# Four first products taken from the input without its norm's factor, with the input read first, in four blocks

## What is computed

```python
h = rms_norm(x, norm1_g[l])
z = h @ w_in[l].astype(h.dtype)
glu_in, q, k, v, gate_logits = jnp.split(z, SPLITS, axis=-1)
a_val, a_gate = jnp.split(glu_in, 2, axis=-1)
a = a_val * jax.nn.sigmoid(a_gate)
a = causal_depthwise_conv(a, conv_w[l], conv_b[l])
```

## Time and profile before

| | us |
|---|---|
| median of 3 runs | 908.16 |
| lowest, highest | 907.64, 909.5 |
| the profiled execution | 906.52 |
| its span in the trace | 904.7 |
| first product with a weight starts | 14.38 |
| first job of q reaches the sum of squares on PE | 97.23 |

### The profile page before, as it was taken

The page is one execution under the profiler, slowest core; times in us unless marked ns, Lnnn a source line. Parts: engine busy times, 40 slices in busy tenths (PEclk is TensorE's granted clock), DMA queues, the critical chain, the costliest instruction groups (busy, mean ns, idle before and its releaser), DMA issues.

```text
span 904.7 us, 18066 instructions
## 1 busy us (share of the span) xinstructions
PE 859.0 (95%) x6762; PEld 837.4 (93%) x6762; DVE 649.4 (72%) x1059; ACT 555.5 (61%) x999; POOL 350.5 (39%) x324
## 2 busy tenths in 40 slices
PE   4999889999999999999999989899999999999996
PEld 3998889999899899999999878799999999999996
DVE  5987999896777798777665659957577854444542
ACT  5677778887646576665555675456645655555441
POOL 3799995435432253333110215701032243333111
PEclk9999999999999999999999999999999999999999
DMA  5655444444565366665656443245345466654741
GB/s 201 209 187 186 162 144 151 137 132 140 151 184 186 111 189 205 186 180 175 214 163 194 160 142 110 82 136 166 115 143 172 150 211 188 182 180 152 217 133 47
DMA packets 42310, 146.41 MB, mean 162 GB/s; under 512 B 4704, under 2 KB 7024, under 8 KB 42224
## 3 DMA queue, kind: packets, MB, share of 16 engines
q1 hardware_dynamic: 41472, 143.67, 50.9%
q10 hardware_dynamic: 752, 1.59, 0.5%
...
## 4 chain that ended last, share of the span: by engine, by line
PE 72%; DVE 11%; issue 8%; POOL 6%; ACT 3%; DMA 1%; DVEq 0%; POOLq 0%; ACTq 0%
PE px L507 22%; PE px L508 22%; PE px L509 22%; DVE wlo L1316 3%; POOL CA L1876 2%; DVE px L1375 2%; POOL att L1996 1%; PE px L549 1%; PE px L571 1%; ACT whi L843 1%; DVE sq L1331 1%; POOL wlo L1827 1%; DVE Q L1406 1%; DMA X<-xs 1%; ACT hx L870 1%
## 5 line engine op out<-in xcount | busy, mean ns | idle before, releaser
L507 PE MATMUL px<-hx,whi 128*128 128x256 f32 x1392 | 404.4, 291 | 9.2 <-DVE hx L1337 6.1
L509 PE MATMUL px<-hx,wlo 128*128 128x256 f32 x1392 | 396.6, 285 | 0.0
L508 PE MATMUL px<-hx,whi 128*128 128x256 f32 x1392 | 396.6, 285 | 0.0
L1316 DVE TENSOR_TENSOR wlo<-raw,whi 128x1024 fp32r<-128x1024 f32 x251 | 330.8, 1325 | 65.0 <-ACT whi L843 64.6
L843 ACT ACTIVATE whi<-raw 128x1024 fp32r<-128x1024 f32 x267 | 279.9, 1051 | 65.0 <-PE px L509 49.8
L507 PEld LDWEIGHTS px<-hx,whi 128*128 128x128 f32 x1392 | 269.7, 194 | 14.2 <-DVE hx L1337 7.4
L508 PEld LDWEIGHTS px<-hx,whi 128*128 128x128 f32 x1392 | 270.0, 194 | 0.4
L509 PEld LDWEIGHTS px<-hx,wlo 128*128 128x128 f32 x1392 | 269.7, 194 | 0.0
L1950 POOL TENSOR_TENSOR fx<-tt,fx 128x256 fp32r<-128x256 f32 x40 | 54.3, 1359 | 130.1 <-ACT fx L1104 130.1
L1876 POOL TENSOR_TENSOR CA<-CA,ct 128x256 f32<-128x256 f32 x90 | 85.7, 953 | 45.5 <-ACT ct L910 37.9
L508 PE MATMUL px<-fx,whi 128*128 128x256 f32 x352 | 99.6, 283 | 0.0
...
## 6 DMA issues: line engine op xcount, KB each, us to landing
raw<-ws SPq DMA_DIRECT2D x267, 512.0 KB, 3.7
...
```

The source lines that it names most:

```text
L507: e.matmul(b[:, 0:S], H, xh, start=first, stop=False)
L508: e.matmul(b[:, 0:S], H, xl, start=False, stop=False)
L509: m = e.matmul(b[:, 0:S], L, xh, start=False, stop=end)
L1316: e.tensor_tensor(wlo[:, n % NSL, :], raw[:, n % NRAW, :], whi[:, n % NSL, :], ALU.subtract).then_inc(s_lov, 1)
```

## The change

The factor 1 / rms is taken out of the first four jobs. ACT makes `ax` high = round(X * gain), DVE the low half, and ag0, av0, ag1, av1 use `ax` in place of `hx`. When rst is there, DVE multiplies their results by it (`early`), and forms the gated tiles in a second step (`early_gated`). `hx` is made as before, for the jobs from ag2 on.

The input is stored as four blocks of two tiles, which SP loads ahead of all else. Chunks 0 and 1 are loaded and split in halves of 512 columns. Of the vector of small constants the first 9 columns come by themselves (through ACT's queue), the rest after chunk 2. Chunk 3's low half moves from POOL to DVE. PE runs 20 products of ones by ones (128 columns, type f32) before its first job; nobody reads the result. The norm's sum on PE stands after av0.

```diff
-s_x = [sem("s_x0"), sem("s_x1")]
+s_x = [sem(f"s_x{i}") for i in range(4)]
 def on_gpsimd(c):
-    return c < 64 and c % 4 == 3
+    return 4 <= c < 64 and c % 4 == 3
...
# PE
+e.wait_ge(s_con, 1)
+for _ in range(WARM):
+    e.matmul(px[VALUES[0]][:, 0:P], ones[:, :], ones[:, :], start=True, stop=True, skip_group_check=True)
+job(("ag", 0), AX, first_gained, rings=(FEW,))
+job(("av", 0), AX, rings=(FEW,))
 sums("n1")
-for i in range(KD):
-    job(("ag", i), HX, normed("n1") if i == 0 else None, rings=(FEW,))
+job(("ag", 1), AX, rings=(FEW,))
+job(("av", 1), AX, rings=(FEW,))
+for i in range(2, KD):
+    job(("ag", i), HX, normed("n1") if i == 2 else None, rings=(FEW,))
     job(("av", i), HX, rings=(FEW,))
...
# ACT
+e.dma_start(vc[:, 0:FIRST_VECS], vecs[:, 0:FIRST_VECS]).then_inc(s_vg, 16)
 e.preload_act_table_set(LOG)
...
 for i in range(KD):
+    if i % 2 == 0:
+        e.wait_ge(s_x[i // 2], 16)
+    e.activation(ax[:, i, 0, :], X[:, i, :], ACT.Copy, scale=vec("norm1_g", i)).then_inc(s_xgh, 1)
+    if i == 5:
+        half_high(0, 0)
+half_high(0, 1)
...
 rms("n1", D)
+def early_gate(i):
+    e.wait_ge(*BANK[("ag", i), 0])
+    e.activation(sg[:, i, :], sg[:, i, :], ACT.Tanh, scale=0.5).then_inc(s_eg, 1)
+early_gate(0)
+highs(4)
+early_gate(1)
+e.wait_ge(s_vc, 16)
+for i in range(KD):
+    e.wait_ge(s_nt, i + 1)
+    e.activation(hx[:, i, 0, :], sq[:, nt_slot("n1", i), :], ACT.Copy).then_inc(s_nhi, 1)
     if i == 4:
+        highs(5)
...
# DVE
+e.wait_ge(s_vg, 16)
+for i in range(KD):
+    e.wait_ge(s_xgh, i + 1)
+    e.scalar_tensor_tensor(out=ax[:, i, 1, :], in0=X[:, i, :], scalar=vec("norm1_g", i), in1=ax[:, i, 0, :],
+                           op0=ALU.mult, op1=ALU.subtract).then_inc(s_xgl, 1)
+    if i == 5:
+        half_low(0, 0)
+half_low(0, 1)
+half_low(1, 0)
+half_low(1, 1)
+lows(2)
...
+def early(key, to):
+    e.wait_ge(s_mm, ENDS[key])
+    e.tensor_tensor(to, px_of[key, 0][:, 0:S], rst[:, 0, 0:S], ALU.mult).then_inc(BANK[key, 0][0], 1)
...
# SP
-e.dma_start(X[:, 4:8, :], xv[:, 4:8, :]).then_inc(s_x[1], 16)
+for i in range(4):
+    tiles(i)
+half_load(0, 0)
+half_load(0, 1)
+half_load(1, 0)
+half_load(1, 1)
+loads(2)
+e.dma_start(vc[:, FIRST_VECS:], vecs[:, FIRST_VECS:]).then_inc(s_vc, 16)
```

More of the change, by code:

```diff
@@ L374, in two_blocks @@
         MX = CX + pairs(mh3, 3)
-        s_x = [sem("s_x0"), sem("s_x1")]
+        s_x = [sem(f"s_x{i}") for i in range(4)]
+        s_vg, s_half = sem("s_vg"), [sem(f"s_half{i}") for i in range(HALVED)]
         s_vc, s_wg2, s_caus, s_msk, s_pos, s_out = (sem(n) for n in (
@@ L423, in on_gpsimd, with steps, half, gated_half @@
         def on_gpsimd(c):
-            return c < 64 and c % 4 == 3
+            return 4 <= c < 64 and c % 4 == 3
+        def steps(c):
+            return 2 if c < HALVED else 1
         LOW = {}
         for c in range(n_chunks):
-            n = c // 4 if c < 64 else 16
-            LOW[c] = (s_log, c // 4 + 1) if on_gpsimd(c) else (s_lov, c + 1 - n)
+            mine = [d for d in range(c + 1) if on_gpsimd(d) == on_gpsimd(c)]
+            LOW[c] = (s_log if on_gpsimd(c) else s_lov, sum(steps(d) for d in mine))
+        HI = [sum(steps(d) for d in range(c + 1)) for c in range(n_chunks)]
+        def half(h):
+            return slice(h * CW // 2, (h + 1) * CW // 2)
+        def gated_half(i):
+            return (s_ci, i + 1) if i < 2 else BANK[("av", i), 0]
         ACC = {i: px[3][:, S * (n % 2):S * (n % 2) + S] for n, i in enumerate(CONV_V)}
@@ L456, in two_blocks @@
         QR = [qraw[:, 12 + n, :] for n in range(4)]
-        xv = x.rearrange("p (k s) -> p k s", k=KD)
+        xv = [x[i * P:(i + 1) * P, :].rearrange("p (k s) -> p k s", k=2) for i in range(KD // 2)]
         outv = out.rearrange("p (k s) -> p k s", k=KD)
@@ L498, in job @@
                     c, o = (at_ + k * w) // CB, (at_ + k * w) % CB * P
-                    if c != seen[0]:
+                    if c < HALVED and o in (0, CW // 2):
+                        e.wait_ge(s_lov, 2 * c + 1 + (o > 0))
+                    elif c >= HALVED and c != seen[0]:
                         seen[0] = c
@@ L832, in _, with half_high @@
         def _(e):
-            made = [0]
+            made = [HALVED]
+            def half_high(n, h):
+                e.wait_ge(s_raw[n] if h else s_half[n], 16)
+                e.activation(whi[:, n, half(h)], raw[:, n, half(h)], ACT.Copy).then_inc(s_hi, 1)
             def highs(c):
@@ L1303, in _, with half_low @@
         def _(e):
-            made = [0]
+            made = [HALVED]
+            def half_low(n, h):
+                e.wait_ge(s_hi, 2 * n + h + 1)
+                e.tensor_tensor(wlo[:, n, half(h)], raw[:, n, half(h)], whi[:, n, half(h)], ALU.subtract).then_inc(s_lov, 1)
             def lows(c):
@@ L1312, in lows @@
                         continue
-                    e.wait_ge(s_hi, n + 1)
+                    e.wait_ge(s_hi, HI[n])
                     if n >= NSL:
@@ L1359, in _, with early_gated @@
             e.tensor_scalar(qg8[:, :], vec("qg"), 0.125, None, ALU.mult).then_inc(s_cst, 1)
-            norm("n1", X, "norm1_g", hx)
+            lows(3)
+            def early(key, to):
+                e.wait_ge(s_mm, ENDS[key])
+                e.tensor_tensor(to, px_of[key, 0][:, 0:S], rst[:, 0, 0:S], ALU.mult).then_inc(BANK[key, 0][0], 1)
+            def early_gated(i):
+                e.wait_ge(s_eg, i + 1)
+                e.wait_ge(*BANK[("av", i), 0])
+                e.scalar_tensor_tensor(out=CI[:, i, 30:], in0=sg[:, i, :], scalar=1.0, in1=CI[:, i, 30:], op0=ALU.add,
+                                       op1=ALU.mult).then_inc(s_ci, 1)
+            e.wait_ge(s_rms, 1)
+            early(("ag", 0), sg[:, 0, :])
+            early(("av", 0), CI[:, 0, 30:])
+            scaled("n1", 0, X[:, 0, :], "norm1_g")
+            early(("ag", 1), sg[:, 1, :])
+            for i in range(1, KD):
+                scaled("n1", i, X[:, i, :], "norm1_g")
+                low_tile("n1", i - 1, hx)
+                if i == 3:
+                    lows(4)
+                elif i == 5:
+                    early_gated(0)
+            low_tile("n1", KD - 1, hx)
+            early(("av", 1), CI[:, 1, 30:])
+            lows(5)
+            early_gated(1)
             def taps(c):
@@ L1382, in _ @@
                 taps(2 * i + 1)
[L1383 to L1386 removed]
+                if i >= 2:
+                    e.wait_ge(*BANK[("ag", i), 0])
+                    e.wait_ge(s_mm, ENDS["av", i])
+                    e.scalar_tensor_tensor(out=CI[:, i, 30:], in0=sg[:, i % 3, :], scalar=1.0,
+                                           in1=px_of[("av", i), 0][:, 0:S], op0=ALU.add, op1=ALU.mult).then_inc(
+                                               BANK[("av", i), 0][0], 1)
             for n in range(2):
@@ L2039, in table, with tiles, half_load @@
                 e.dma_start(tb[:, h % 3, :], tabs[h]).then_inc(s_tb[h % 3], 16)
-            e.dma_start(X[:, 4:8, :], xv[:, 4:8, :]).then_inc(s_x[1], 16)
+            def tiles(i):
+                e.dma_start(X[:, 2 * i:2 * i + 2, :], xv[i]).then_inc(s_x[i], 16)
+            def half_load(n, h):
+                e.dma_start(raw[:, n, half(h)], ws[n][:, half(h)]).then_inc(s_raw[n] if h else s_half[n], 16)
+            for i in range(4):
[6 more added lines that the diff above has]
+            e.dma_start(vc[:, FIRST_VECS:], vecs[:, FIRST_VECS:]).then_inc(s_vc, 16)
             loads(ahead(last_chunk(QKG[9])) + NRAW)
```

63 lines of the change are left out of this document (34 added, 29 removed).

## The result

| | before | after |
|---|---|---|
| median | 907.78 us | 913.01 us |
| lowest, highest | 906.73, 909.5 | 912.25, 915.43 |
| the profiled execution's span | 904.7 | 911.2 |
| first product with a weight | 14.38 | 8.82 |
| first tap on POOL | 34.70 | 37.97 |

The changed kernel is slower: ratio 1.0061, 95% interval 1.0046 to 1.0077, or 5.2 us. PE starts 5.6 us earlier, and the kernel ends later. Only 9 of the 124 are as short as before's profiled execution (906.52); their common median is 909.03. So a shift against that one trace looks up to 2.5 us worse than one against a usual execution of before.

A forecast was written before the change was run, and what follows sets the result against it. POOL, then DVE, bound the kernel up to 131.5 us, not PE, so POOL's first tap sets the end. Variants +1.6 and +2.8 gave a middle of 2.2: 908.16 + 2.2 = 910.4 us, range 905.5 to 913.0.

The forecast's parts named there:

- 1.6 for the taps: POOL's first tap at 36.5 instead of 34.7, 1.8 later, 1.6 with 0.2 taken off, passed on to the end.
- 0.6 for half of a low clock at the start: Clock falling in PE's wait behind av0 puts the end at +2.8 instead of +1.6; the middle, 2.2, was taken.
- Input and ACT: Span's start: first `ax` at 3.9, chunk 2's high half at 11.9, its low half at 13.1, additions ending at 16.1.
- the idle time behind av0: PE, from 13.4 to 16.1: it waits 2.7 us for the norm's additions.
- From rst to POOL's last low tile: Norm tiles on ACT, DVE and POOL: from rst at 18.2 to the last low tile at 29.2, instead of 20.07.
- the row by which the forecast went: ACT's profile row: table load 1.28 us, tanh 0.01 after it; the skill's further 1.38 drain would give 911.8.
- The 0.2 us taken off for POOL's one wait: POOL's single 0.4 us wait for ACT: about 0.2 isn't its ordinary tap step, so the end moves that much less.
- The clock at the start: PE's 2.7 us wait behind av0: if the clock falls, sum and ag1 lose some 1.5 us, ACT hides 0.3.
- PE at 97 us: PE's wait ahead of `hsq`: longer than before, first `hsq` product at 98.8 or later instead of 97.23.
- PE's gain getting through: Faster rival, chance 0.15: POOL has unseen slack, PE's 2.6 us gain at av3 remains, 905.6, down to 904.2.
- Warm products that don't warm: Slower rival, chance 0.07: low clock for ag0 and av0, 10.2 us not 5.8; end 2.7 later than forecast, 913.1.
- Nothing is left either way: Rival, chance 0.18: POOL and DVE hold each other up; another phase can give back one or two us, 908.2.

The follow-up runs named there:

- the 124: Executions of the unchanged kernel before, timed 124 times on four chips beside the follow-up experiments; medians 908.53 to 909.23 us, common median 909.03.
- the one with 14 products filled in: Changed kernel with 14 unread products of ones on PE ahead of its first `hsq` product: 910.31 us against 909.23 for before, ratio 1.0015.
- three kernels: 14 products filled in: changed kernel 1.0015 (unfilled 1.0061), with norm's chain first 0.9975 (0.9991), with chain and POOL's memsets first 0.9968 (0.9994).

## Why the prediction was too low

The direction and the core hold: PE's start gives nothing, POOL's first tap is late, and its delay reaches the end whole. The time is 913.01 where 910.4 was forecast, with 913.0 as the upper end. The forecast's 2.2 us were 1.6 for the taps and 0.6 for half of a low clock at the start. Measured are 3.3 for the taps, none for the second term in the profiled execution, and a rest that the forecast has no term for. Step by step:

- *Input and ACT.* First `ax` at 3.70 (forecast 3.9). But a rounding with the gain costs 0.40 us in a row, not 0.31, the third block came at 5.83 instead of 5.1 and the first half piece at 7.32 instead of 6.3. So chunk 2's high half ends at 13.1 instead of 11.9, its low half at 14.36 instead of 13.1, the additions end at 17.34 instead of 16.1, `rst` at 19.55 instead of 18.2. **This term was mis-sized by 1.35 us.** On 0.40: the Trainium skill, "ScalarE: Activation LUTs", What ACT_TABLE_LOAD costs, gives 93 ns for each per-partition operand; 0.31 and 0.09 make the 0.40 of the trace.
- *PE.* ag0 starts at 8.82 (7.6 to 8.7), and the idle time behind av0 is 2.83 us (2.7).
- *From rst to POOL's last low tile.* 11.1 us (11.0). The table load takes 1.28 us and tanh starts 0.01 us behind it, as in the row by which the forecast went.
- *POOL.* The memsets 4.9 and the low half 2.4 as counted. 37.97 instead of 36.5, which is `rst`'s delay. The 0.2 us taken off for POOL's one wait wasn't there: 3.3 at the first tap, 3.4 at 126 us.
- *The clock at the start.* In this execution it stayed up at the sum and fell at 26.3. In others it fell at the sum (at 17.0 in the one with 14 products filled in), and the first tap came at 39.15, 1.2 later: the step that the forecast priced at 1.2 and took half of.
- *PE at 97 us.* The forecast said that PE "waits longer at chunk 15 and at 97 us" and gave the longer wait no price. **This is the step that was missing.** The earlier trace rows showed a fall behind a wait of nearly 3 us; the same rule was used for the wait at 14 us and not for the one at 97, though its own delay of 1.6 us makes 3.2 of the 1.60 there. Executions with the fall end 2.8 to 4.1 us behind where their taps put them; filling the wait took 2.2 to 2.7 us off the medians of three kernels.

The sum with both: 3.3 for the taps and 3.1 for the fall are 6.4 in the profiled execution (6.5 seen), while the medians differ by 5.2, and by 3.8 to 4.5 against the medians of before's 124 executions. How the medians divide is not settled. Taps that are 3.6 us late in the kernel before cost 3.6 and not 6.9, and with the wait filled the changed kernel is only 0.15% (1.4 us) slower, though its taps still come over 3 us late. Both would follow if a usual execution of before lost some 2.5 us that its profiled one didn't. The times and granted clocks of the 124 bear this out in part: the 38 with a mean clock of 0.986 or 0.987 have a median of 909.5, the 49 with 0.988 or 0.989 have 908.5, the 27 with 0.990 or more have 908.1, and the profiled one (0.990) took 906.5. Where a usual execution loses the time no trace shows; only one of before was kept.

Of the rivals, PE's gain getting through fell: POOL's taps show no idle time beside them. Warm products that don't warm fell, the clock rose at 5.85. "Nothing is left either way" fell too: that POOL and DVE hold each other up was right as a mechanism and wrong in sign, since the changed phase cost time and gave none back.
